# Attention in steps of two heads with stationary values in a two-block transformer kernel

## The reference

```
# A: 4 heads, each with two components of 64; values of 128 per head
logits = einsum('bqhcd,bkhcd->bhcqk', q, ka) * 64**-0.5      # causal
p = softmax(logits)
attn = p[:, :, 0] - lam * p[:, :, 1]
out_a = rmsnorm(einsum('bhqk,bkhe->bqhe', attn, va), g_sub_a) * (1 - lam_init)   # per head of 128
# B: 8 heads of 64, keys selected by an index score (128 per query)
p = softmax(where(valid, einsum(q, k_selected) * 64**-0.5, -inf))
out_b = einsum(p, v_selected)
y = concatenate([out_a, out_b]) @ w_out
```

## Time and profile before

| | |
|---|---|
| median of 3 runs | 3101.69 us (3094.66 to 3102.46) |
| profiled execution | 3105.4 us |
| its span | 3103.7 us |
| TensorE busy | 2888.8 us, 93% |
| VectorE / ScalarE busy | 778.7 / 442.2 us |
| moved by DMA | 570.75 MB, mean 184 GB/s |
| mean granted TensorE clock | 0.976 |

### The profile page before, as it was taken

One profiled execution on the slowest core, in us unless ns is written; L12 is line 12 of the kernel. 1 busy time (PEld: TensorE's weight loads), 2 busy tenths in 40 slices (PEclk: granted clock), 3 DMA queues, 4 the chain that ended last, 5 costly groups with the idle time before them and its releaser, 6 DMA issues. The chain is left out here.

```text
span 3103.7 us, 25172 instructions
## 1 busy us (share of the span) xinstructions
PE 2888.8 (93%) x9875; PEld 1323.0 (43%) x9875; DVE 778.7 (25%) x2032; ACT 442.2 (14%) x934; POOL 56.7 (2%) x149
## 2 busy tenths in 40 slices
PE   8998889999999999999999899798999899899888
PEld 4544544444444445444544444464433233233232
DVE  3398523101001214240000244544111111111111
ACT  2123412100001003211000122242000000000000
POOL 0000000000000000110000010000000000000000
PEclk9998999999999999999999999898999999999999
DMA  7230011212222111582112111213899999999998
GB/s 274 68 109 14 1 40 54 83 61 75 81 82 84 56 54 55 174 282 102 65 64 72 54 56 55 75 39 126 346 427 428 428 429 429 428 428 428 429 427 375
DMA packets 107475, 570.75 MB, mean 184 GB/s; under 512 B 11578, under 2 KB 12364, under 8 KB 82940
## 3 DMA queue, kind: packets, MB, share of 16 engines
q1 hardware_dynamic: 99248, 538.64, 43.2%
q0 software_dynamic: 6768, 29.43, 2.8%
q10 hardware_dynamic: 1372, 1.51, 0.1%
HBM read 567.43 MB, written 6.32 MB: 185 GB/s over the span
## 5 line engine op out<-in xcount | busy, mean ns | idle before, releaser
L205 PE MATMUL banks<-hT,ring 128*128 128x512 f32 x1024 | 441.5, 594 | 5.1 <-PEq L298 5.1
L205 PEld LDWEIGHTS banks<-hT,ring 128*128 128x128 f32 x1024 | 195.0, 191 | 250.4 <-issue 250.4
L2823 PE MATMUL banks<-ring,second_arena 128*64 128x512 f32 x1024 | 232.0, 597 | 29.7 <-DMA ring<-in_w_up 16.0
L1890 PE MATMUL banks<-ring,second_arena 128*128 128x512 f32 x512 | 222.6, 597 | 0.0
L324 PE MATMUL banks<-ring,m_u 128*128 128x512 f32 x512 | 220.3, 592 | 1.6 <-PEq L178 1.6
L2823 PE MATMUL banks<-second_arena 128*64 128x512 f32 x768 | 174.5, 598 | 17.4 <-DMA second_arena<-in_w_gate 15.0
L1890 PEld LDWEIGHTS banks<-ring,second_arena 128*128 128x128 f32 x512 | 98.2, 192 | 123.0 <-issue 123.0
L324 PEld LDWEIGHTS banks<-ring,m_u 128*128 128x128 f32 x512 | 97.0, 190 | 123.4 <-issue 123.4
L2823 PEld LDWEIGHTS banks<-ring,second_arena 128*64 128x64 f32 x1024 | 70.0, 136 | 184.0 <-issue 133.5
L2823 PE MATMUL banks<-ring,mod 128*64 128x512 f32 x512 | 114.7, 596 | 13.1 <-DMA ring<-in_w_down 13.1
L2943 DVE TENSOR_TENSOR x_rows<-banks,x_rows 128x512 f32<-128x512 f32 x64 | 44.2, 691 | 282.4 <-PE banks L2859 282.4
(11 more groups left out here) (578 smaller groups left out, 3027.7 us busy)
## 6 DMA issues: line engine op xcount, KB each, us to landing
ring<-in_w_up SPq DMA_DIRECT2D x48, 2048.0 KB, 30.7
ring<-in_w_down SPq DMA_DIRECT2D x48, 2048.0 KB, 33.8
ring<-in_w_gate SPq DMA_DIRECT2D x32, 2048.0 KB, 34.0
second_arena<-in_w_gate SPq DMA_DIRECT2D x32, 2048.0 KB, 30.7
second_arena<-in_w_down SPq DMA_DIRECT2D x24, 2048.0 KB, 35.4
second_arena<-in_w_up SPq DMA_DIRECT2D x16, 2048.0 KB, 32.4
hT<-in_w_up SPq DMA_DIRECT2D x16, 2048.0 KB, 33.8
second_arena<-in_w_ada POOLq DMA_DIRECT2D x32, 768.0 KB, 4.8
```

What stands on the lines that cost most here:

```text
L205: mm = nc.tensor.matmul(o, w[:, k, a:z], src[:, ka, 0:ntok], start=(ka == 0), stop=(ka == kc * kgroups - 1))
L1890: mm = nc.tensor.matmul(g.psum[:, b * NT + m, :], u[:, ka, m * P:m * P + P], w[:, k, :], start=(ka == 0), stop=(ka == KD * kgroups - 1))
L2823: mm = nc.tensor.matmul(g.psum[64 * e:64 * e + 64, bank, :], lhs(q * half + k)[:, 64 * e:64 * e + 64], w[:, e, k, :], start=first, stop=last)
```

## The change

`attend` is replaced by `attend_steps`. A step is one tile of 128 queries of two score rows of 64 features, which lie on partitions 0 to 63 and 64 to 127: two heads in B and in the dilated attention, the two components of one head in A (`apart`). The transposed probabilities go through one pair of banks (4 and 5, one per head of the step). ScalarE copies the first head's always and the second's on even steps, and VectorE the second's on odd steps. They are collected in `keyed` with two query tiles side by side.

For steps that aren't `apart`, the values are stationary (64 columns), the probabilities of two query tiles move (256 columns), and the two heads' results lie on the two halves of the partitions of one bank. The result is transposed already and is copied straight into `g.hT`. The probabilities are scaled by the reciprocal sums before the transposes. For A's steps the transposed probabilities stay stationary; both components are transposed and multiplied with the values apart, and VectorE forms the difference from the two results in PSUM.

A and B of the first mixer are one call with lag 3, so that one barrier and one warm-up are gone. The output norm of A is inside it: squares on ScalarE, the root by VectorE's integer method (`rsqrt`) in step 22, the scaling in steps 23 to 26, the gain as a column factor of the final copies, and 16 transposes near the end. The dilated attention has lag 2. `close_parts` loses its transposes and their copies.

```diff
-def attend(g, name, units, comps, width, out_evac, mask_scale, warm=0, space=None):
...
+def attend_steps(g, name, steps, probs, keyed, scale, lag, warm=5, rows=None):
+    S, B = len(steps), 4
+    ops = []
+    for s, step in enumerate(steps):
+        if step["opens"]:
+            ops.append([])
+        ops[-1].append(s)
+    op_of = [v for v, group in enumerate(ops) for _ in group]
+    last_of = {group[-1]: v for v, group in enumerate(ops)}
+    mixed_before = [sum(not st["apart"] for st in steps[:s + 1]) for s in range(S)]
+    s_scores, s_peak, s_probs, s_mixed, s_turned, s_out, s_read, s_copied_a, s_copied_v = (g.counter(n) for n in (
+        "scores", "peak", "probs", "mixed", "turned", "out", "out_read", "moved_a", "moved_v"))
...
+    def wait_copied(eng, s):
+        eng.wait_ge(*s_copied_a.at(copied_by_act(s)))
+        if s:
+            eng.wait_ge(*s_copied_v.at(copied_by_dve(s)))
+    def into(s, e):
+        step = steps[s]
+        n = step["nk"] // P
+        at = 0 if step["apart"] else (s - ops[op_of[s]][0]) * P
+        return (keyed[op_of[s] % 2][:, e, 0:n, at:at + P],
+                g.psum[:, 4 + e, 0:step["nk"]].rearrange("p (j q) -> p j q", q=P))
...
+                def turn(s):
+                    step = steps[s]
+                    if step["apart"]:
+                        pe.wait_ge(*s_probs.at(s + 1))
+                    else:
+                        pe.wait_ge(*s_mixed.at(mixed_before[s]))
+                    if s:
+                        wait_copied(pe, s - 1)
+                    for e in range(2):
+                        for j in range(step["nk"] // P):
+                            mm = nc.tensor.transpose(g.psum[:, 4 + e, j * P:j * P + P], probs[:, s % B, e, j * P:j * P + P],
+                                                     g.ident[:])
+                        mm.then_inc(s_turned.up(), 1)
+                def values(v):
+                    step = steps[ops[v][-1]]
+                    wait_copied(pe, ops[v][-1])
+                    if v >= 2:
+                        pe.wait_ge(*s_read.at(v - 1))
+                    n = step["nk"] // P
+                    held = keyed[v % 2]
+                    if step["apart"]:
+                        for e in range(2):
+                            for j in range(n):
+                                mm = nc.tensor.matmul(g.psum[:, 6 + v % 2, e * P:e * P + P], held[:, e, j, 0:P],
+                                                      step["v"][j], start=(j == 0), stop=(j == n - 1))
+                    else:
+                        for j in range(n):
+                            a = step["from"][j]
+                            for e in range(2):
+                                mm = nc.tensor.matmul(g.psum[64 * e:64 * e + 64, 6 + v % 2, a:2 * P], step["v"][e][j],
+                                                      held[:, e, j, a:2 * P], start=(j == 0), stop=(j == n - 1))
                     mm.then_inc(s_out.up(), 1)
-                        nc.tensor.matmul(g.psum[:, 7, :], g.ident[:], g.causal[:, 0:BANK], start=True, stop=True)
+                for s in range(S + lag + 1):
+                    if s < S:
+                        scores(s)
+                    if s == 0:
+                        for _ in range(warm):
+                            nc.tensor.matmul(g.psum[:, 7, :], g.ident[:], g.causal[:, 0:BANK], start=True, stop=True)
+                    if 0 <= s - lag < S:
+                        turn(s - lag)
+                    if s - lag - 1 in last_of:
+                        values(last_of[s - lag - 1])
+                    if rows and s == S:
+                        pe.wait_ge(*s_peak.at(S))
+                        pe.wait_ge(*s_scaled.at(NT))
+                        for c in range(4):
+                            for i in range(NT):
+                                mm = nc.tensor.transpose(g.psum[:, c, i * P:i * P + P], rows["x"][:, i, c * P:c * P + P],
+                                                         g.ident[:])
+                            mm.then_inc(s_rows_turned.up(), 1)
...
+                def mix(s):
+                    step = steps[s]
+                    if step["apart"]:
+                        return
+                    dve.wait_ge(*s_probs.at(s + 1))
+                    g.vlink(v_.reciprocal(st[:, s % 8, 3, :], st[:, s % 8, 2, :]))
+                    for e in range(2):
+                        p = probs[:, s % B, e, 0:step["nk"]]
+                        ins = v_.tensor_scalar(p, p, st[:, s % 8, 3, e:e + 1], None, ALU.mult)
+                    ins.then_inc(s_mixed.up(), 1)
+                def copy_turned(s):
+                    dve.wait_ge(*s_turned.at(2 * s + 2))
+                    if op_of[s] >= 2:
+                        dve.wait_ge(*s_out.at(op_of[s] - 1))
+                    v_.tensor_copy(*into(s, 1)).then_inc(s_copied_v.up(), 1)
+                def finish(v):
+                    step = steps[ops[v][-1]]
+                    ps = g.psum[:, 6 + v % 2, :]
+                    if not step["apart"]:
+                        dve.wait_ge(*s_out.at(v + 1))
+                        v_.tensor_copy(step["out"], ps[:, 0:2 * P]).then_inc(s_read.up(), 1)
+                        return
+                    r = st[:, v % 8, 3, :]
+                    dve.wait_ge(*s_probs.at(v + 1))
+                    g.vlink(v_.reciprocal(r, st[:, v % 8, 2, :]))
+                    g.vlink(v_.tensor_tensor(r, r, signs, ALU.mult))
+                    dve.wait_ge(*s_out.at(v + 1))
+                    g.vlink(v_.tensor_scalar(step["out"], ps[:, 0:P], r[:, 0:1], None, ALU.mult))
+                    v_.scalar_tensor_tensor(step["out"], ps[:, P:2 * P], r[:, 1:2], step["out"], ALU.mult,
+                                            ALU.add).then_inc(s_read.up(), 1)
+                def row_scale():
+                    dve.wait_ge(*s_squared.at(apart))
+                    g.vlink(v_.tensor_scalar(mean, total, 1.0 / P, EPS, ALU.mult, ALU.add))
+                    rsqrt(g, rstd, mean, total)
+                def scale_rows(i):
+                    x = rows["x"][:, i, :].rearrange("p (h d) -> p h d", d=P)
+                    v_.tensor_tensor(x, x, rstd[:, 4 * i:4 * i + 4].unsqueeze(2).to_broadcast([P, 4, P]),
+                                     ALU.mult).then_inc(s_scaled.up(), 1)
...
+                for s in range(S + lag + 2):
+                    if s < S:
+                        peak(s)
+                    if 1 <= s <= S:
+                        mix(s - 1)
+                    if 0 <= s - lag < S and (s - lag) % 2:
+                        copy_turned(s - lag)
+                    if s - lag - 2 in last_of:
+                        finish(last_of[s - lag - 2])
+                    if rows:
+                        if s == apart + lag + 3:
+                            row_scale()
+                        if apart + lag + 4 <= s < apart + lag + 4 + NT:
+                            scale_rows(s - apart - lag - 4)
...
+                def square(v):
+                    act.wait_ge(*s_read.at(v + 1))
+                    if v:
+                        act.wait_ge(*s_squared.at(v))
+                    h, i = divmod(v, NT)
+                    nc.scalar.activation(gains[:, 0:P], steps[v]["out"], ACT.Square,
+                                         accum_out=total[:, 4 * i + h:4 * i + h + 1]).then_inc(s_squared.up(), 1)
...
+                for s in range(S + lag):
+                    if s < S:
+                        exponent(s)
+                    if s >= lag:
+                        copy_turned(s - lag, 0)
+                        if not (s - lag) % 2:
+                            copy_turned(s - lag, 1)
+                    if rows and 0 <= s - lag - 3 < apart:
+                        square(s - lag - 3)
...
+            steps += [dict(apart=False, opens=i % 2 == 0, nk=(i + 1) * P,
+                           q=[QTb[64 * e:64 * e + 64, h, i * P:i * P + P] for e in range(2)],
+                           k=[KTb[64 * e:64 * e + 64, h, 0:(i + 1) * P] for e in range(2)],
...
+                           v=[[vb[:, j, (2 * h + e) * 64:(2 * h + e) * 64 + 64] for j in range(i + 1)] for e in range(2)],
+                           **{"from": [0] * i + [P]},
+                           out=g.hT[:, 4 + h, (i - 1) * P:(i + 1) * P]) for h in range(4) for i in range(NT)]
+            probs = g.sb("e_probs", [P, 4, 2, BANK], ctx=c2)
+            keyed = [g.sb(f"e_keyed{b}", [P, 2, 4, 2 * P], ctx=c2) for b in range(2)]
+            attend_steps(g, "e_att", steps, probs, keyed, 64 ** -0.5, 3,
+                         rows=dict(x=ya, gain=g.gain["g_sub_a"], factor=0.8, out=g.hT[:, 0:4, :]))
+        add_and_turn(g, g.hT, col(g, "g_xattn", 0))
...
-        pool.wait_ge(*ya_turned.at(NT))
...
-        for c in range(NT):
-            for i in range(NT):
-                mm = nc.tensor.transpose(g.psum[:, 4 + c, i * P:i * P + P], ya[:, i, c * P:c * P + P], g.ident[:])
-            mm.then_inc(ya_turned.up(), 1)
```

(14 more changed lines are left out.)

225 lines of the change are left out of this document (78 added, 147 removed).

## The result

| | before | after |
|---|---|---|
| median | 3102.07 us (3094.66 to 3103.60, 4 runs) | 3049.95 us (3047.22 to 3052.72, 4 runs) |
| ratio, 95% interval | | 0.9835 (0.9818 to 0.9852) |
| span of the profiled execution | 3103.7 us | 3045.5 us |

The account below looks back on a forecast made before the run. TensorE, busy 93% of the span, was taken to set the pace up to the experts' fixed-length weight stream. Savings of 17 (second attention) and 28 (first mixer) make 45 us, giving 3057 us against the median 3101.69; range 3034 to 3082.

Parts of the forecast that it names:

- Second attention: Dilated attention in 16 steps of two heads: 7.7 us per two steps against 9.9, 17 us saved.
- The microsecond charged for the clock: Second attention: one microsecond taken off its saving for the clock, leaving 17 us.
- The values of one operation: Value matmuls of two steps, second attention: 1.75 us for 16 records, 1.95 with tile-size change; bounds 1.0 to 3.5.
- the two column halves: Value matmuls: halves run together at 256 columns; rival that they don't: 23 us more, 3080, chance 0.04.
- Attention A: First mixer: 3.0 us per step, no faster than now; twelve steps from 274.4 to 310.4.
- 42.4 + 3: B, first mixer: 42.4 us for 16 steps, plus 3 us of norm work that VectorE's slack doesn't hide.
- B's own round: B, first mixer: 5.3 us per two steps, 2.65 apart.
- the 4 us charged for a falling clock: First mixer: 4 us added to its end because the clock falls now and then.
- its 28: First mixer: output projection's first matmul at 373 against 401.3, 28 us saved.
- The clock rivals: Both attention stretches: mean clock 0.80 gives 3070, chance 0.13; half clock throughout gives 3118, chance 0.05.
- Engine sums: Rival, both stretches: engine work sums set the pace, 6.0 us per two steps in second attention; 3031, chance 0.12.
- One-for-one passage: Whole kernel: a microsecond saved in either attention is one of the total; rival, 17 us absorbed: 3074, chance 0.03.

Follow-up runs that it names:

- e2: The kernel before with the steps of two heads in the second (dilated) attention only, first mixer as before; 3087.05 us, ratio 0.9949.
- e8: The changed kernel run again unaltered, for the spread between executions; 3055.75 us, ratio 0.9845.
- e7: The changed kernel with attention A, its norm and row transposes in the old form, and B in steps in its own block; 3071.05 us.
- e6: The changed kernel without the output norm's root and with only one column per head scaled; 3048.20 us, ratio 0.9825.
- e4: The changed kernel with ScalarE's copies of turned probabilities issued ahead of its exponentials; 3037.68 us, ratio 0.9788.
- e5: e4 with VectorE's copy also moved ahead of its scaling, and lag 3 in the second attention; 3035.14 us, ratio 0.9779.
- e10: e5 with the norm's four scalings moved from VectorE to GpSimd; 3035.44 us, ratio 0.9782.
- e9: The changed kernel without the five warm-up matmuls in each of the two new blocks; 3044.26 us, ratio 0.9816.
- e11: e5 without the warm-up matmuls; 3023.97 us, ratio 0.9729.

## Why the prediction was right, and where it was off

**Second attention: 17 forecast, 18.8 measured** (18.1 in e2, 15.1 in e8). The start to step 1's peaks was 0.9 shorter than forecast (9.1 us from the first score matmul, not 10.0). From step 1's peaks to step 5's 12.7 us (12.8 forecast), five rounds 38.5 (38.5), from there to the next block's matmuls 11.3 (11.0 with its waits). The microsecond charged for the clock was not needed in this execution, and in e8 it was 3.7. The values of one operation, the price with the widest bounds (1.0 to 3.5), are 1.95 as taken; the two column halves do run together with 256 columns.

**Attention A: right.** 36.8 us for twelve steps (36.0 forecast), and 11.99 for four of them, 3.0 each, "no faster than now". The odd rounds are the long ones.

**B: the step that was mis-sized.** 48.0 us for 16 steps where 42.4 + 3 had been forecast. B's own round was right: in e7, where B has neither A's tail nor the norm in it, four steps take 10.43, 2.61 a step for 2.65 forecast. Two terms fell short. The norm costs 4.0 and not 3 over the 16 steps (e6). And the 16 steps without it take 44.0, not 42.4: the steps from 15 to 22 are 2.86 apart, 1.5 us too much in all, and they hold the tail of A, which I had put down to A. Each of the last of A's operations is finished on VectorE five steps late, a scaling and a multiply-add of 0.35 and the small ones before them; in step 17 VectorE has no idle time at all. That these outputs are what lengthens the steps is not shown: ScalarE's squares and A's last transposes and values fall in the same steps, and with the copies first the same steps are 2.68 (e4) and 2.64 (e5) apart with all of A's outputs still in them. Together 1.0 for the norm and 1.6 for the tail are the 2.6 that B was longer than forecast. Two of A's outputs (L696, L697) around step 17's peaks and scaling:

```profile
315.79 0.35 DVE L696 TENSOR_SCALAR e_qb<-banks,e_att_stats 128x128 f32<-128x128 f32 x1
...
316.18 0.35 DVE L697 SCALAR_TENSOR_TENSOR e_qb<-banks,e_att_stats,e_qb 128x128 f32<-128x128 f32 x1
316.45 0.41 DVE L661 CUSTOM_DVE_ANT_0 e_probs<-banks,e_bias 128x256 f32<-128x256 f32 x1
...
317.52 0.48 DVE L675 TENSOR_SCALAR e_probs<-e_probs,e_att_stats 128x128 f32<-128x128 f32 x2
...
318.30 0.35 DVE L696 TENSOR_SCALAR e_qb<-banks,e_att_stats 128x128 f32<-128x128 f32 x1
...
318.69 0.35 DVE L697 SCALAR_TENSOR_TENSOR e_qb<-banks,e_att_stats,e_qb 128x128 f32<-128x128 f32 x1
318.96 0.55 DVE L661 CUSTOM_DVE_ANT_0 e_probs<-banks,e_bias 128x384 f32<-128x384 f32 x1
```

**Start and clock: two misses that paid for B.** The warm-up in front of A took 4.56 us, not the 6.59 of the earlier trace rows, because it ran at a granted clock of 1.00 (0.68 before), so the start is 2.3 shorter. That is luck in part: in e10 the same ten records took 6.58 at 0.68. And the 4 us charged for a falling clock weren't used: the window is at 0.97. The forecast's terms come to 108.6 from the first score matmul; less 2.3 and 4, plus 0.8 in A and 2.6 in B, with the drain as forecast (13.0), is 105.7, and 105.7 came. The forecast is thus better founded in the second attention than in the first mixer, where errors of 2 to 4 us stood against each other, and the 3.4 us by which that stage beat its 28 are no more than the clock that was charged and not used.

**The clock rivals** didn't come. The window that was at 0.50 before, inside A, is at 0.76 after (276 to 282), and A as a whole went from 0.80 to 0.97 with twice as many transposes in it. The Trainium skill, "TensorE: Matmul & The Clock Gate", Part 4, says that transposes don't count as busy for the gate. The traces here don't agree with it. A's rise to 0.97 alone would prove little, since its value records doubled with the transposes. But the kernel before has a stretch in which TensorE runs nothing else, and the forecast, which had only the first sixteen of it, left it open. TensorE had been idle for 12.16 us, then ran 32 transposes; the granted clock is 0.50 at first and 1.00 from 398.8 on, in the midst of them, and the second sixteen take 2.24 where the first took 3.65 (timeline, then windows as above):

```profile
398.12 2.24 PE L465 MATMUL banks<-ident,e_kb 128*128 128x128 f32 x16
```

```profile
394.70:398.70 4.00, 4.00 (x19) 4.00 (x20) 1.38 (x2) 0.94 (x2) 0.00 (x0) 0.50 0.01 2
398.80:400.40 1.60, 1.56 (x14) 1.32 (x12) 1.13 (x2) 0.76 (x3) 0.00 (x0) 1.00 0.00 0
```

The same rise within transposes shows in e2 and e7. e9 and e11 have a granted clock of 0.94 or more without any warm-up matmul. How low the clock falls still differs from one execution to the next (e8, e10).

**Engine sums.** The rival was named with 6.0 us per two steps (less than the 6.2 that the forecast itself gives TensorE), 2.5 a step in A and 2.3 in B. It was wrong for this change, because of the order of work. e5, with the two copies moved forward, comes near it: 6.31, 2.56 a step in A, and 2.2 in B's last four, though with the norm and A's tail all 16 of B's steps take 44.8, 2.8 each. The Trainium skill's remark ("TensorEngine Tiling (Array Packing)", PSUM Bottleneck), that tiling leaves emptying PSUM as it was, is met in part. In after it is not the copying itself that binds, since VectorE has 5.8 and ScalarE 4.7 of work in 7.70 us, but where the copies stand in each engine's order. In e5 VectorE with its peaks, scalings and copies sets B's last steps, 27 to 31, in which it is never idle.

**One-for-one passage.** Shown by the last stages, 86.2 to 86.3 and 929.8 to 932.0 us in all thirteen profiles, whatever went before them.

**What the profile of before couldn't give.** The 10 us of the stretch between belong to the execution, not the change. By the two attention stages the gain is 50.2 us in one profile of the kernel after and 46.5 in the other, where 45 had been forecast. The ends of the range, 3034 and 3082, don't follow from the forecast's own terms, which give 3031 for the engine sums and 3079 on the slow side; the measured 3050 lies well inside both.
